# New opening and group tables, eviction one half later, taps by tile pairs, and a silu on ScalarE in a one-layer streaming encoder

## What is computed

```python
xn = rmsnorm(x); z = xn @ w_in            # u (512) | conv GLU p, q (2 x 512) | gates (2048)
y, h = s5(u)                              # diagonal complex state space, scan over time
pa, qa = split(gelu(y) @ w_ssm_glu);      branch_a = pa * sigmoid(qa)
v = p * sigmoid(q)                        # then a causal depthwise convolution, 31 taps
c = silu(layernorm(conv(v) + conv_b));    branch_b = c @ w_conv_out
x = x + (sigmoid(ga) * branch_a + sigmoid(gb) * branch_b) @ w_out
# PEER: 8 heads, 128 x 128 product keys, top 16 experts of 16384
s1, s2 = q[0] @ k1.T, q[1] @ k2.T         # 16 best of each, then 16 best sums
x = x + sum_k softmax(sc)_k * gelu(u_tab[e_k] . xn2) * v_tab[e_k]
```

## Time and profile before

| | |
|---|---|
| median of the timed runs | 3581.9 us |
| the profiled execution: time, span | 3598.6 us, 3596.6 us |
| PE, DVE, ACT, POOL busy | 3197.2, 2433.1, 1409.6, 1401.1 us |
| moved by DMA | 1336.4 MB, mean 372 GB/s |
| gathers of experts | 1088, 1140.9 MB |
| mean granted TensorE clock | 0.962 of full |
| first Gelu of dots (end of the opening) | 343.0 us |

### The profile page before, as it was taken

How to read it: one execution, slowest core, us unless ns; L and a number is a source line. 1 busy time by engine, 2 the same in 40 slices (tenths; PEclk the granted TensorE clock), 3 DMA queues, 4 the chain that set the end, 5 groups by cost and what they waited for, 6 DMA issues and landing times.

```text
span 3596.6 us, 33769 instructions
## 1 busy us (share of the span) xinstructions
PE 3197.2 (89%) x10016; PEld 1828.4 (51%) x10016; DVE 2433.1 (68%) x5507; ACT 1409.6 (39%) x4197; POOL 1401.1 (39%) x1240
## 2 busy tenths in 40 slices
PE   7888999999999998999999998999999877777776
PEld 6676555555555555555655555555655322322232
DVE  6633579777656689777656588777666666666674
ACT  4312444554333344554333444554333333333332
POOL 1101445333343444333333344434333444454443
PEclk9899998999999998999999998999999999999999
DMA  4257998999999998999999997999999999999998
GB/s 135 72 169 239 380 418 334 367 419 379 419 405 417 410 405 321 376 410 389 419 405 404 404 407 291 389 409 400 419 409 405 409 420 420 394 420 414 414 403 348
DMA packets 232071, 1336.42 MB, mean 372 GB/s; under 512 B 27664, under 2 KB 49296, under 8 KB 92624
## 3 DMA queue, kind: packets, MB, share of 16 engines
q0 software_dynamic: 156672, 1140.92, 78.0%
q1 hardware_dynamic: 62992, 179.96, 13.7%
q10 hardware_dynamic: 12224, 13.38, 1.0%
HBM read 1310.93 MB, written 23.23 MB: 371 GB/s over the span
## 4 chain that ended last, share of the span: by engine, by line
PE 61%; DMA 20%; ACT 8%; DVE 5%; issue 5%; POOL 1%; POOLq 0%; SPq 0%; DVEq 0%; ACTq 0%
PE ps_acc L757 33%; DMA rows<-in_experts,idx 19%; PE ps_a L593 15%; PE ps_v L593 5%; PE ps_a L668 3%; DVE rows L1363 2%; ACT uy L814 2%; POOL rows L1509 1%; PE ps_y L635 1%; ACT coef L908 1%; ACT diag L912 1%; PE ps_a L695 1%; DVE va L1208 1%; ACT L905 1%; PE ps_a L672 1%
## 5 line engine op out<-in xcount | busy, mean ns | idle before, releaser
L757 PE MATMUL ps_acc<-rows,diag 128*128 128x512 f32 x4352 | 2052.8, 620 | 319.8 <-ACT diag L912 316.6
L1509 POOL DMA_INDIRECT rows<-in_experts,idx x1088 | 1272.5, 1170 | 1878.4 <-PE ps_acc L757 1516.9
L1363 DVE CUSTOM_DVE_ANT_0 rows<-rows,xn 128x1024 f32<-128x1024 f32 x1088 | 1331.1, 1233 | 845.8 <-DMA rows<-in_experts,idx 832.4
L757 PEld LDWEIGHTS ps_acc<-rows,diag 128*128 128x128 f32 x4352 | 839.9, 198 | 1370.3 <-issue 862.7
L905 ACT ACTIVATE act_v<-dots 128x2 f32<-128x2 f32 x544 | 109.8, 202 | 1170.0 <-DVE dots L1363 1158.2
L912 ACT ACTIVATE diag<-pk,coef 128x128 f32<-128x128 f32 x1088 | 377.2, 394 | 17.7
L593 PE MATMUL ps_a<-xnT,ring 128*128 128x272 f32 x1536 | 375.1, 400 | 0.9 <-ACT xnT L802 0.7
L593 PEld LDWEIGHTS ps_a<-xnT,ring 128*128 128x128 f32 x1536 | 297.5, 194 | 93.1 <-issue 35.0
L908 ACT ACTIVATE coef<-act_v,soft 128x1 f32<-128x1 f32 x1088 | 261.4, 287 | 17.8
L593 PE MATMUL ps_a<-gates,ring 128*128 128x272 f32 x1024 | 247.7, 395 | 4.2 <-issue 3.4
L1208 DVE SCALAR_TENSOR_TENSOR va<-va,pk 128x302 f32<-128x302 f32 x480 | 247.1, 579 | 1.9
(11 more groups left out here) (224 smaller groups left out, 2240.6 us busy)
## 6 DMA issues: line engine op xcount, KB each, us to landing
ring<-in_slabs SPq DMA_DIRECT2D x256, 512.0 KB
rows<-in_experts,idx POOLq DMA_INDIRECT x1088
ring<-made_slabs SPq DMA_DIRECT2D x24, 512.0 KB
sc<-score_rows SPq DMA_DIRECT2D x68, 128.0 KB
score_rows<-gp ACTq DMA_DIRECT2D x32, 256.0 KB
xt<-in_x_prompt SPq DMA_DIRECT2D x4, 1024.0 KB
x_rows<-xt ACTq DMA_DIRECT2D x4, 1024.0 KB, 11.6
x2t<-x_rows SPq DMA_DIRECT2D x8, 512.0 KB
```

The source lines that it names most:

```text
L757: ins = pe.matmul(ps_acc[:, h, :], diag[:, slot, :], rows[:, slot, D + h * 512:D + (h + 1) * 512], start=first, stop=False, skip_group_che ...
L1363: ins = dve.tensor_tensor_reduce(rows[:, slot, 0:D], rows[:, slot, 0:D], xn[:, :], 1.0, 0.0, ALU.mult, ALU.add, dots[:, s:s + 1])
L1509: pool.indirect_dma_start(out=rows[:, slot, :], out_offset=None, in_=experts, in_offset=bass.IndirectOffsetOnAxis(ap=idx[:, a, k:k + 1], a ...
```

## The change

Both tables are new. In STEADY the taps start at half 11 instead of 18, in units of two taps by two channel tiles (units 0 to 15 for tiles 0 and 1, units 16 to 31 for tiles 2 and 3), a half with a `turn_in` has no unit, and the `s` steps stand at 12, 16, 24 and 28, the `y` steps at 20, 24, 32 and 36. `Plan` has a field `lag`: 0 for the opening and 1 for the groups, by which ACT evicts every ps_a product (but not `xn`) one half after PE makes it. The steps mean to out come three or four halves earlier, those of rows, q and score one to three. In the opening, three gates move ahead of the GLU slabs, the y steps are three halves apart, the taps begin at half 10, mean and var move to halves 29 and 32 and OPEN is 59. Layer norm still takes ACT's root and DVE's reciprocal; the sigmoid on ACT and the shaping and product on DVE become one silu on ACT, with scale and bias operands, written straight into `cs`. SP loads the first scores two halves after that head's last score product, and the first rows one q later. DVE's `cout` step waits for the last gate.

```diff
@@ -82,8 +82,8 @@
 class Plan:
-    def __init__(self, pe, other, streamed):
-        self.pe, self.other = pe, other
+    def __init__(self, pe, other, streamed, lag):
+        self.pe, self.other, self.lag = pe, other, lag
         self.a, self.v, self.slab, self.slabs = {}, {}, {}, []
         a = v = 0
         for h in range(HALVES):
@@ -108,36 +108,39 @@
 OPENING = Plan(
     {"xn": [0], "u": [1, 2, 3, 4], "cq": [5, 7, 9, 11], "cp": [6, 8, 10, 12],
-     "s": [10, 12, 14, 16], "y": [14, 16, 18, 20],
-     "gate": [13 + m for m in range(10)] + [31 + m for m in range(6)], "glu": [23 + j for j in range(DT)],
-     "mean": [32], "var": [34], "cout": [38, 39, 40, 41], "out": [43 + j for j in range(DT)],
-     "rows": [52, 53, 54], "q": [51 + m for m in range(2 * HEADS)],
-     "score": [52 + m for m in range(2 * HEADS)]},
+     "s": [10, 12, 14, 16], "y": [15, 18, 21, 24],
+     "gate": [13 + m for m in range(13)] + [34 + m for m in range(3)], "glu": [26 + j for j in range(DT)],
+     "mean": [29], "var": [32], "cout": [37, 38, 39, 40], "out": [42 + j for j in range(DT)],
+     "rows": [51, 52, 53], "q": [50 + m for m in range(2 * HEADS)],
+     "score": [51 + m for m in range(2 * HEADS)]},
     {"cp": [7, 9, 11, 13], "turn_in": [11, 13, 15, 17], "scan": [11, 13, 15, 17], "turn_back": [11, 13, 15, 17],
-     "gelu": [15, 17, 19, 21], "tap": [15 + k // 2 for k in range(TAPS)], "glu": [24 + j for j in range(DT)],
-     "centre": [33], "square": [33], "eps": [35], "root": [35], "scale": [36], "swish_in": [36], "swish": [37],
-     "cout": [39, 40, 41, 42], "rows": [53, 54, 55], "sq": [55], "ms2": [56], "rs": [57],
-     "load_x": [60], "sq_next": [64], "ms_next": [65], "norm_next": [66]}, False)
+     "gelu": [16, 19, 22, 25], "tap": [10, 10, 12, 12, 14, 14, 16, 16] + [18 + u // 2 for u in range(24)],
+     "glu": [27 + j for j in range(DT)],
+     "centre": [30], "square": [30], "eps": [33], "root": [33], "scale": [34], "swish": [35],
+     "cout": [38, 39, 40, 41], "rows": [52, 53, 54], "sq": [54], "ms2": [55], "rs": [56],
+     "load_x": [59], "sq_next": [63], "ms_next": [64], "norm_next": [65]}, False, 0)
 STEADY = Plan(
-    {"xn": [0], "u": [17, 19, 21, 23], "cq": [1, 5, 9, 13], "cp": [3, 7, 11, 15],
-     "s": [20, 22, 24, 26], "y": [26, 28, 30, 32],
-     "gate": [25 + 2 * m for m in range(10)] + [44] + [61 + 2 * m for m in range(5)],
+    {"xn": [0], "u": [9, 11, 21, 23], "cq": [1, 5, 13, 17], "cp": [3, 7, 15, 19],
+     "s": [12, 16, 24, 28], "y": [20, 24, 32, 36],
+     "gate": [25 + 2 * m for m in range(10)] + [44, 54] + [61 + 2 * m for m in range(4)],
      "glu": [45 + 2 * j for j in range(DT)],
-     "mean": [52], "var": [58], "cout": [71, 73, 75, 77], "out": [80 + 2 * j for j in range(DT)],
-     "rows": [95, 97, 99], "q": [96 + 2 * m for m in range(2 * HEADS)],
-     "score": [97 + 2 * m for m in range(2 * HEADS)]},
-    {"cp": [5, 9, 13, 17], "turn_in": [22, 24, 26, 28], "scan": [22, 24, 26, 28], "turn_back": [22, 24, 26, 28],
-     "gelu": [27, 29, 31, 33], "tap": [18 + k for k in range(TAPS)], "glu": [47 + 2 * j for j in range(DT)],
-     "centre": [54], "square": [55], "eps": [60], "root": [61], "scale": [62], "swish_in": [63], "swish": [65],
-     "cout": [73, 75, 77, 79], "rows": [97, 99, 101], "sq": [101], "ms2": [102], "rs": [104],
-     "load_x": [106], "sq_next": [117], "ms_next": [119], "norm_next": [121]}, True)
+     "mean": [48], "var": [54], "cout": [68, 70, 72, 74], "out": [77 + 2 * j for j in range(DT)],
+     "rows": [94, 96, 98], "q": [93 + 2 * m for m in range(2 * HEADS)],
+     "score": [95 + 2 * m for m in range(2 * HEADS)]},
+    {"cp": [6, 10, 18, 22], "turn_in": [14, 18, 26, 30], "scan": [14, 18, 26, 30], "turn_back": [14, 18, 26, 30],
+     "gelu": [21, 25, 33, 37],
+     "tap": [11, 12, 13, 15, 16, 17, 19, 20, 21, 22, 23, 24, 25, 27, 28, 29] + [31 + u for u in range(16)],
+     "glu": [48 + 2 * j for j in range(DT)],
+     "centre": [51], "square": [52], "eps": [57], "root": [58], "scale": [60], "swish": [62],
+     "cout": [70, 72, 74, 76], "rows": [96, 98, 100], "sq": [101], "ms2": [102], "rs": [104],
+     "load_x": [106], "sq_next": [117], "ms_next": [119], "norm_next": [121]}, True, 1)
 A_ALL, V_ALL = OPENING.a_all, OPENING.v_all
 SLABS_0, SLABS_G = len(OPENING.slabs), len(STEADY.slabs)
 SLABS = SLABS_0 + (GROUPS - 1) * SLABS_G
 SKEW = 4
-OPEN = 60
+OPEN = 59
 ALL_TURNS = TILES * TPAIRS * PTURNS + SPAIRS * PTURNS
 LAST_PAIR = TILES * TPAIRS + SPAIRS - 1
...
@@ -492,11 +494,11 @@
                     sp.wait_ge(made_stored, 96)
                 mix(h, 0)
-                if h == OPENING.pe["q"][5]:
-                    for b in range(2):
+                for b in range(2):
+                    if h == OPENING.pe["score"][2 * b + 1] + 2:
                         sp.wait_ge(score_out[b], 32)
                         load_scores(0, b)
-                if h == OPENING.pe["q"][7]:
+                if h == OPENING.pe["q"][8]:
                     sp.wait_ge(rows_out, 32)
                     sp.wait_ge(rs_out, 48)
                     load_rows(0)
@@ -832,8 +834,12 @@
                     act.dma_start(sc_s[g, h // 4, h % 4], scsb[0:NS, b, 2, :]).then_inc(score_out[b], 16)
             def mix(h, g):
-                at, due = plan(g).at, plan(g).due
-                for _ in at("xn", h):
+                due = plan(g).due
+
+                def at(piece, h):
+                    return plan(g).at(piece, h - plan(g).lag)
+
+                for _ in plan(g).at("xn", h):
                     to_channels(a_at(g, "xn"), "norm_mix", g)
                 for m in at("u", h):
                     cross(uS[:, m, :], ready(a_at(g, "u", m)), ACT.Copy, False).then_inc(a_done, 1)
@@ -857,11 +863,14 @@
                 for _ in due("root", h):
                     v_emptied(v_at(g, "var"))
                     act.activation(lnr[1][:, 0:NC], lnr[0][:, 0:NC], ACT.Sqrt).then_inc(std_ready, 1)
-                for _ in due("swish_in", h):
+                for _ in due("swish", h):
+                    act.wait_ge(y_done, CT * (g + 1) + 2)
                     act.wait_ge(ln_ready, g + 1)
                     for c in range(CT):
-                        act.activation(sq[:, c, :], acc[:, c, :], ACT.Sigmoid, bias=par("ln_b")[:, c:c + 1],
-                                       scale=par("ln_g")[:, c:c + 1]).then_inc(ln_sig, 1)
+                        out, shape = by_step(cs[:, c, :]), (par("ln_b")[:, c:c + 1], par("ln_g")[:, c:c + 1])
+                        act.activation(out[:, :, 0:KP], in_time(acc[:, c, 0:NP]), ACT.Silu, bias=shape[0], scale=shape[1])
+                        act.activation(out[:, :, KP:NK], in_time(acc[:, c, SOFF:NC]), ACT.Silu, bias=shape[0],
+                                       scale=shape[1]).then_inc(cs_ready, 1)
                 for j in at("out", h):
                     src = ready(a_at(g, "out", j))[:, 0:N]
                     act.activation(outT[:, j, :], src, ACT.Copy)
@@ -1195,20 +1204,23 @@
             before = [0] * CT
-            def tap(k):
-
-                taps = par("conv_w")
-                for c in range(CT):
-                    src, wk = vbuf[:, c, k:k + NC], taps[:, c * TAPS + k:c * TAPS + k + 1]
-                    if k == 0:
-                        before[c] = mark(dve.tensor_scalar(acc[:, c, :], src, wk, par("conv_b")[:, c:c + 1],
-                                                           ALU.mult, ALU.add))
-                    else:
-                        after(before[c])
-                        last = dve.scalar_tensor_tensor(acc[:, c, :], src, wk, acc[:, c, :], ALU.mult, ALU.add)
-                        if k < TAPS - 1:
-                            before[c] = mark(last)
-                if k == TAPS - 1:
+            def tap(unit, g):
+
+                taps, (two, first) = par("conv_w"), divmod(unit, 16)
+                if first == 0:
+                    emptied(v_at(g, "cp", 2 * two + 1))
+                for k in range(2 * first, min(2 * first + 2, TAPS)):
+                    for c in (2 * two, 2 * two + 1):
+                        src, wk = vbuf[:, c, k:k + NC], taps[:, c * TAPS + k:c * TAPS + k + 1]
+                        if k == 0:
+                            before[c] = mark(dve.tensor_scalar(acc[:, c, :], src, wk, par("conv_b")[:, c:c + 1],
+                                                               ALU.mult, ALU.add))
+                        else:
+                            after(before[c])
+                            last = dve.scalar_tensor_tensor(acc[:, c, :], src, wk, acc[:, c, :], ALU.mult, ALU.add)
+                            if unit < 31 or k < TAPS - 1:
+                                before[c] = mark(last)
+                if unit == 31:
                     last.then_inc(conv_ready, 1)
             def glu(j, g):
@@ -1244,8 +1256,8 @@
                     turn_in(t, g)
                 for t in due("scan", h):
                     scan(t, g)
-                for tap_k in due("tap", h):
```

(15 more changed lines are left out.)

## The result

The changed kernel takes 3499.2 us (median of 4 runs, 3498.2 to 3500.5), the one before in the same session 3581.7 (4 runs, 3570.3 to 3587.0): a ratio of 0.977, 95% interval 0.975 to 0.980, or 82.5 us less. The forecast was 102 less, 3480; 3499 lies inside its own range. The gain is made of other shares than I gave it: of 27 us forecast for the opening about 13 came, of 75 for the groups some 65. In the profiled execution the first Gelu of dots starts at 334.1 us; 316 was forecast.

The account below looks back on a forecast made before the run. Steady turns were taken as bound by DMA at 420 GB/s, the opening by PE's work and waits. Opening 27 (11.8 + 11 + 4) plus steady 75 (60 + 15) gave 102 us off 3581.9: 3480, own range 3455 to 3505.

Parts of the forecast that it names:

- What bounds the kernel: Whole kernel: steady turns are bound by DMA at 420 GB/s; mixing groups can give 108 us where the rate falls.
- Steady: eviction later: Mixing groups: evicting one half later ends ACT's wait for PE; 7.4 us of PE cover over 4.4 of ACT work.
- rival E: Mixing groups: table loads between the two batches are exposed, making the kernel slower, 3763 us (half of them: 3655); chance 0.04.
- Steady: the slow stretch: Halves 12 to 35 of each mixing group: 20 us back of 30, 60 in all, bounds 39 to 84.
- Steady: layer norm: Halves 60 to 71 of each mixing group: 5 of 6 us back, 15 in all, bounds 6 to 18.
- Opening: PE's waits: Opening: PE's waits for ACT fall from 24.4 us to 12.6, so 11.8 us back.
- Opening: the clock: Opening: PE's lowered clock costs 14 us, of which 11 come back with shorter waits; bounds 0 and 14.
- Opening: scores sooner: Opening's end: earlier score loads start the choice of experts sooner, 4 us taken; bounds 0 and 4.4.
- B: Halves 12 to 31 of the groups: DVE with POOL's rotation is the new bound, 17 us stay, 3515 us; chance 0.18.
- C: Whole kernel: all the excess goes, 31 + 84 + 18 = 133 us, 3449 us; chance 0.10.
- D: Groups' slow stretch is not cured; only opening and half of layer norm come, 35 us, 3547 us; chance 0.06.
- F: Whole kernel: nothing moves, since PE is as full as DMA, 3582 us; chance 0.02.

Follow-up runs that it names:

- only the opening: Changed kernel's opening, with the group table, taps, swish and eviction (no lag) of the kernel before: 3565.2 us, ratio 0.996 to the kernel before.
- the kernel with both edits: Kernel after, with the opening's first rows loaded one q sooner and its gelu of y taken in the half of y: 3470.8 us, ratio 0.969.
- both runs on the rotation: Kernel after, second half of POOL's rotation in groups 1 to 3 done twice: 3521.8 us, ratio 0.983; left out: 3488.0 us, ratio 0.975.

## Why the prediction was right, and where its steps were off

**What bounds the kernel.** Right. Time was to be had where the rate falls below 420 GB/s, and it came from nowhere else: the part without mixing is as long as it was (the lead stays at 97.4 us from its start on).

**Steady: eviction later.** Right in its mechanism. The cover held: PE does not wait more for diagonals (291.4 against 316.6), and rival E, table loads exposed between batches, did not happen. What I had not seen is that lag and tables are not a sum. I gave the chain and DVE's load as causes of one trough and priced their end together; had only one of them been changed I would have credited it too much, and the tables alone would have cost.

**Steady: the slow stretch.** Forecast 20 us a group, from an excess of 30 of which 10 stays. After, 154.7 us at 397 GB/s would be 146.2 at 420: 8.5 stay in the first group, 9.7 and 9.6 in the others. Measured with halves 36 to 59, which give a part back, halves 12 to 59 went from 319.5, 321.6 and 325.0 us in the profiled execution of before to 300.3, 301.6 and 300.5: 63.7 for the 60 forecast. But against the kernel "only the opening" (320.0, 319.1 and 315.3) it is 52. The size was right for the execution I read and 8 too large for the median that I took it off: I had said that its 17 us above the median belonged to no stage that the change touches. By the kernel "only the opening" the groups held all of them, with 11.5 us in these halves and 8.6 in halves 72 to 127.

**Steady: layer norm.** Forecast 15, bounds 6 to 18. From 72.1, 72.6 and 72.2 to 68.9, 68.3 and 68.3: 11.4. The silu, in the opening:

```profile
208.12 1.28 ACT L871 ACT_TABLE_LOAD   x1
209.41 0.84 ACT L871 ACTIVATE uy<-va,pk 128x256 f32<-128x256 f32 x1
210.16 0.40 ACT L872 ACTIVATE uy<-va,pk 128x16 f32<-128x16 f32 x1
...
213.26 0.40 ACT L872 ACTIVATE uy<-va,pk 128x16 f32<-128x16 f32 x1
213.67 1.28 ACT L851 ACT_TABLE_LOAD   x1
```

From 209.41 to 213.66 it takes 4.3 us for the forecast 3.0: the pieces of 16 columns, with scale and bias, cost 0.40, not the 0.27 that I took from a copy with a scale alone, and the long ones 0.83. It costs nothing all the same, as the run without it shows. No drain shows after the table load here either: the silu starts 0.01 us after it.

**Opening: PE's waits.** Right. Of 24.4 us forecast to become 12.6, these stand (PE in 70 to 205 us, then the start of the conv projection):

```profile
PE ps_y L634 <- ACT uy L816: 5.7, 3, 1.9
PE ps_a L595 <- ACT uy L816: 5.6, 1, 5.6
```
```profile
213.71 14.93 PE L595 MATMUL ps_v<-uy,ring 128*128 128x272 f32 x64 [2.46 <-ACT uy L872]
```

5.7 for 5.4, 5.6 for 5.5, 2.5 for 1.7: 13.8 in all.

**Opening: the clock.** This step failed, and with it a sign that I had named for being wrong, an opening that still has its low clock. I took 11 of 14 us; 4.5 came. Windows from 83 us to the start of out, before and after:

```profile
83.00:244.00 161.00, 136.12 (x591) 113.47 (x589) 98.90 (x214) 41.52 (x104) 17.74 (x26) 0.89 0.30 91
```
```profile
83.00:230.00 147.00, 131.62 (x590) 108.94 (x589) 92.36 (x194) 46.16 (x110) 19.47 (x27) 0.93 0.32 98
```

For the same products PE is busy 136.1 us before, 131.6 after and 122.1 in the kernel with both edits (its row above). That puts the whole price of the low clock at 14, as I had it, and two thirds of it stayed, since the engine was at 1.2 GHz again after each of the three waits of 1.9 us. PE in the opening of after:

```profile
109.31 0.44 PE L634 MATMUL ps_y<-uy,rows 128*128 128x68 f32 x2 [1.90 <-ACT uy L816]
109.58 0.64 PE L637 MATMUL ps_y<-hst,rows 128*128 128x68 f32 x4
110.03 0.63 PE L634 MATMUL ps_y<-uy,rows 128*128 128x68 f32 x2
110.45 1.06 PE L637 MATMUL ps_y<-hst,rows 128*128 128x68 f32 x4
...
113.86 12.70 PE L595 MATMUL ps_a<-xnT,ring 128*128 128x272 f32 x48
```

The first matmuls after the wait are at full rate (0.64 for four), those from 110.0 on at half (1.06), and three gates take 12.70 us for 11.2. I had written that the waits would be a third of the old and the clock would follow them down; in the rows it does not follow in proportion: the waits before y fell from 14.9 to 5.7 us, and the price of the clock from 14 to 9.5. The trace of before could have warned of it, since its lowered clock also came behind a wait and lasted into the gates.

**Opening: scores sooner.** Forecast 4. The start of out is 14.9 us sooner than before and the first gather 18.8: 3.9 more. But group 1 starts only 13.0 sooner, and 5.8 were lost between. SP, POOL and ACT of after show it:

```profile
308.59 1.19 POOL L1513 DMA_INDIRECT rows<-in_experts,idx  x1 [13.61 <-DVE idx L1343]
...
317.56 0.94 POOL L1513 DMA_INDIRECT rows<-in_experts,idx  x1 [0.30 <-issue]
```
```profile
314.02 0.42 SPq L461 DMA_DIRECT2D rst<-inverse_roots  x1
```
```profile
327.49 0.30 ACT L903 ACTIVATE neg_top<-best,rst 128x2 f32<-128x2 f32 x1 [14.15 <-DMA rst<-inverse_roots]
```
```profile
PE ps_a L595 <- ACT sig L891: 12.9, 1, 12.9
```

The scores now come sooner and the rows later, so inverse_roots is asked for at 314.0, when five gathers of 1 MB have been given out from 308.6 on and three more follow by 317.6, and lands among them at 327.4. ACT stands for it 14.2 us with the eviction of q behind it, PE stands 12.9 us for that, and the clock falls to 0.84 in the window 308 to 352 above. I had seen the load move past a product ("a second from the last use") and priced it against its last use, not against the queue that it would find. This is the other step that failed: the 4 came at the first gather, but the later rows, put at nothing beside it, cost 5.8, so that the term as a whole lies below its bound of 0. I had not asked what the gathers do to a small load issued behind them.

**The sum.** 27 was 11.8 + 11 + 4; it was 9.5 (idle time of PE in the two windows, 24.9 to 15.4) + 4.5 + some 5 more by the first gather (0.9 beyond the windows' ends and 3.9 for the scores), less 5.8: 13. And 75 was 60 + 15; it was 52 + 11.4 in the profiles, and 66 timed. The bounds of the opening, 12 to 31, do not come out of their terms: with the 4 us for a delayed mean and all bounds low they are 11.8 - 4, some 8, and with all high 11.8 + 14 + 4.4, some 30. The total was right with luck in it: the opening gave half of its 27, and the range of 3455 to 3505 was wide enough for that. **The rivals.** B's mechanism is shown by both runs on the rotation, at a size near my forecast's (8.5 to 9.7 us a group) and not near B's 17. C's opening, 31 us, is reached with two entries changed (the first Gelu is then 35 us sooner than before), C's groups are not. D and F are out.

## What to carry to other kernels

Where the order across engines is written by hand, evict a product one place later than it is made, so that the engine that also serves the critical loop does not stand for the matmul, and choose the places anew with it: the tables alone lost time, and the lag alone gave a little over half. A short wait in a dense run of matmuls can cost more than its length: here three of 1.9 us went together with some 9 us of slower products. When a chain is started sooner, look for the small load that its next step needs, and issue it well ahead of the first large gathers, not behind them.

## What was not expected of the hardware

- Three idle times of 1.9 us on TensorE, each between products of 7.5 us and more, went with stretches at 1.2 GHz; without them the granted clock was 0.98 instead of 0.89 over the same 80 us, and the same products up to out took PE 122.1 us instead of 131.6.
- A load of inverse_roots took 13.4 us from issue to landing when it stood behind five gathers of 1 MB, and 10.4 us when it was given out 1.5 us ahead of the first of them.
- An ACTIVATE of 16 columns with scale and bias from memory took 0.40 us; a copy of 16 columns with a scale alone 0.27.
- Time saved in one stretch came back in part in the next one, 4 of 20 us (three groups) with the rotation's half left out, under the same tables. Against the kernel "only the opening" it was 20 of 72, but there the new table had also moved products and slab loads into halves 36 to 59; with the lag alone it was 3 of 39.
